# A two-block kernel's first twenty microseconds: silu(c) spread by TensorE, wider squares, products of ones, another order of loads

## The reference, cut to what matters

```python
cs = jax.nn.silu(c)                                  # c: 1 x 1024
shift, scale, gate = jnp.split(cs @ mod_w[layer] + mod_b[layer], 3, axis=-1)
h = rmsnorm(x, norm_g[layer]) * (1.0 + scale[:, None, :]) + shift[:, None, :]
u, g = jnp.split(h @ rg_w_in, 2, axis=-1)            # then conv, gates, linear recurrence, output product
```

## Time and profile before

| | |
|---|---|
| median of 3 runs | 742.0 us (741.99 to 742.11) |
| profiled execution | 742.27 us, its span 740.5 us |
| TensorE busy | 715.0 us, 97% of the span |
| VectorE, ScalarE busy | 502.9 us, 396.5 us |
| DMA, mean over the span | 212 GB/s |

### The profile page before, as it was taken

How to read it: one execution, slowest core, us unless ns; L and a number is a source line. 1 busy time by engine, 2 the same in 40 slices (tenths; PEclk the granted TensorE clock), 3 DMA queues, 4 the chain that set the end, 5 groups by cost and what they waited for, 6 DMA issues and landing times.

```text
span 740.5 us, 9710 instructions
## 1 busy us (share of the span) xinstructions
PE 715.0 (97%) x3902; PEld 625.0 (84%) x3902; DVE 502.9 (68%) x801; ACT 396.5 (54%) x620; POOL 2.4 (0%) x8
## 2 busy tenths in 40 slices
PE   2999999999999999999999999999999999999996
PEld 1888889999899999888888888888878888888885
DVE  4889996999876879976754454555576544555444
ACT  4156545883874776658734434443666344344423
POOL 0000000000000000000000000000000000000000
PEclk9999999999999999999999999999999999999999
DMA  8999994699835342433755545554336445545201
GB/s 336 419 422 415 421 385 163 250 393 340 316 118 216 116 170 71 182 111 150 271 183 183 208 177 177 207 185 171 114 114 227 171 173 208 187 173 201 81 0 58
DMA packets 23229, 156.65 MB, mean 212 GB/s; under 512 B 2576, under 2 KB 2832, under 8 KB 5264
## 3 DMA queue, kind: packets, MB, share of 16 engines
q1 hardware_dynamic: 22608, 153.41, 55.0%
q0 software_dynamic: 576, 2.62, 0.9%
HBM read 154.97 MB, written 1.05 MB: 211 GB/s over the span
## 4 chain that ended last, share of the span: by engine, by line
PE 86%; DVE 8%; ACT 4%; issue 1%; DMA 1%; SPq 0%; DVEq 0%
PE pb L1578 20%; PE pb L1580 20%; PE pb L1579 20%; PE pb L1642 13%; DVE w L1017 3%; DVE raw L1020 2%; PE pb L1852 2%; PE pb L1963 1%; PE pb L1719 1%; PE pb L1718 1%; PE pb L1720 1%; DMA x<-x_dram 1%; ACT w L624 1%; PE pb L1638 1%; PE pb L1885 1%
## 5 line engine op out<-in xcount | busy, mean ns | idle before, releaser
L1017 DVE TENSOR_TENSOR w<-raw,w 128x2048 fp32r<-128x2048 f32 x97 | 221.3, 2291 | 141.1 <-ACT w L624 141.1
L624 ACT ACTIVATE w<-raw 128x2048 fp32r<-128x2048 f32 x97 | 184.7, 1912 | 135.8 <-PE pb L1580 114.7
L1578 PE MATMUL pb<-w,r 128*128 128x512 f32 (+1 forms) x640 | 244.7, 382 | 0.7 <-DVE r L1020 0.3
L1580 PE MATMUL pb<-w,r 128*128 128x512 f32 (+1 forms) x640 | 241.1, 377 | 0.0
L1579 PE MATMUL pb<-w,r 128*128 128x512 f32 (+1 forms) x640 | 240.7, 376 | 0.0
L1578 PEld LDWEIGHTS pb<-w,r 128*128 128x128 f32 x640 | 120.5, 188 | 23.3 <-issue 2.1
L1580 PEld LDWEIGHTS pb<-w,r 128*128 128x128 f32 x640 | 120.4, 188 | 22.5
L1579 PEld LDWEIGHTS pb<-w,r 128*128 128x128 f32 x640 | 120.6, 188 | 21.0
L1578 PE MATMUL pb<-r,w 128*128 128x256 f32 x288 | 82.5, 287 | 0.4 <-DVE r L1017 0.4
L1579 PE MATMUL pb<-r,w 128*128 128x256 f32 x288 | 81.5, 283 | 0.0
L1580 PE MATMUL pb<-r,w 128*128 128x256 f32 x288 | 81.5, 283 | 0.0
(11 more groups left out here) (203 smaller groups left out, 657.2 us busy)
## 6 DMA issues: line engine op xcount, KB each, us to landing
raw<-w_dram SPq DMA_DIRECT2D x129, 1024.0 KB, 4.9
ow<-w_dram SPq DMA_DIRECT2D x8, 1024.0 KB, 14.2
ow<-w_dram SPq DMA_DIRECT2D x8, 512.0 KB, 17.0
oh<-w_dram SPq DMA_DIRECT2D x2, 1024.0 KB, 23.1
x<-x_dram SPq DMA_DIRECT2D x2, 512.0 KB, 6.1
f<-rc_dram POOLq DMA_DIRECT2D x1, 1024.0 KB, 5.1
acc<-row_dram POOLq DMA_DIRECT2D x2, 512.0 KB, 6.8
out_dram<-f SPq DMA_DIRECT2D x4, 256.0 KB, 2.3
```

Of the source, the lines that this page charges most:

```text
L624: return e.activation(out, in_, ACT.Copy, **kw)
L1017: return e.tensor_tensor(out, a, b, op)
L1578: e.matmul(out, a_hi, b_hi, start=start, stop=False)
L1580: return e.matmul(out, a_lo, b_hi, start=False, stop=stop)
```

## The change

- The load of c and its silu over 128x1024 go. The column silu(c), 128x8, which ScalarE computed already, is spread by TensorE: eight products with the identity into two banks, and VectorE copies the two banks of 128x512 into the same place (`silu_c`).
- The squares: one ScalarE instruction for tiles 0 to 3, two of two tiles each for the rest, into `F1`. VectorE adds two tiles at a time: three adds of 128x512 and one of 128x256, with the two copies of silu(c) between the first and the second.
- `first_close(0)` stands behind `first_tile(0)`. The table for the root is loaded before the squares.
- TensorE multiplies ones with ones where it has nothing to do: three products of 128x256 before the spreads of silu(c), four behind them, one behind the row sums and three behind the spread of the norm.
- The list of loads: first 0 and 1, u0, first 2, u1, first 3, u2, first 4, u3, first 5 and 6, u4, first 7, u5, u6, u7.

```diff
-    for kt in range(KT):
-        plan.extend([("first", "mod_w", 0, kt), ("u", "rg_w_in", 0, kt)])
+    for kind, kts in (("first", (0, 1)), ("u", (0,)), ("first", (2,)), ("u", (1,)), ("first", (3,)), ("u", (2,)),
+                      ("first", (4,)), ("u", (3,)), ("first", (5, 6)), ("u", (4,)), ("first", (7,)), ("u", (5, 6, 7))):
+        plan.extend((kind, "rg_w_in" if kind == "u" else "mod_w", 0, kt) for kt in kts)
...
     o = Outputs()
+    o.place(1, ("sc", 0))
+    o.place(2, ("sc", 1))
+    o.finish(("sc", 0), ("sc", 1))
...
             e.dma_start(cst[:, 0:P], cst_d[:, 0:P]).then_inc(s_id, 16)
-            e.dma_start(acc[0][:, :], c_d).then_inc(s_c, 16)
...
             e.activation(sm[:, 0, :], V("c", 0, 8), ACT.Silu).then_inc(s_cs, 1)
-            p.wait_ge(s_c, 16)
-            e.activation(silu_c, silu_c, ACT.Silu).then_inc(s_silu, 1)
-            for kt in range(KT):
-                if kt % 4 == 0:
-                    p.wait_ge((s_xa, s_xb)[kt // 4], 16)
-                e.activation(tt[kt][:, :], X[:, kt, :], ACT.Square).then_inc(s_sq, 1)
 
             e.activation(rn[:, 0, :], V("eps", 0, 2), ACT.Sqrt)
+            p.wait_ge(s_xa, 16)
+            e.activation(F1[:, 0:4, :], X[:, 0:4, :], ACT.Square).then_inc(s_sq0, 1)
+            p.wait_ge(s_xb, 16)
+            for kt in (4, 6):
+                e.activation(F1[:, kt:kt + 2, :], X[:, kt:kt + 2, :], ACT.Square).then_inc(s_sq0, 1)
...
-            e.memset(ones, 1.0).then_inc(s_ones, 1)
+            e.memset(ones, 1.0)
+            e.memset(sqt[0][:, :], 1.0).then_inc(s_ones, 1)
...
-            for kt in range(1, KT):
-                p.wait_ge(s_sq, kt + 1)
-                if kt > 1:
-                    p.wait_ge(s_n0, kt - 1)
-                tt_(tt[0][:, :], tt[0][:, :], tt[kt][:, :], ADD).then_inc(s_n0, 1)
+            two = F1[:, 0:2, :]
+            p.wait_ge(s_sq0, 1)
+            tt_(two, two, F1[:, 2:4, :], ADD).then_inc(s_n0, 1)
+            for c in range(2):
+                p.wait_ge(*ended("sc", c))
+                e.tensor_copy(silu_c[:, c * 512:c * 512 + 512], bank_of("sc", c)[:, :]).then_inc(s_silu, 1)
+            for n in range(1, 3):
+                p.wait_ge(s_sq0, n + 1)
+                p.wait_ge(s_n0, n)
+                tt_(two, two, F1[:, 2 * n + 2:2 * n + 4, :], ADD).then_inc(s_n0, 1)
+            p.wait_ge(s_n0, 3)
+            tt_(F1[:, 0, :], F1[:, 0, :], F1[:, 1, :], ADD).then_inc(s_n0, 1)
+            p.wait_ge(s_xb, 16)
             first_sums(0, [0])
             p.wait_ge(s_rt, 1)
             e.reciprocal(c0[:, :], c0[:, :]).then_inc(s_rc0, 1)
             first_sums(0, [1])
-            first_close(0)
             p.wait_ge(s_rs, 1)
             first_tile(0)
+            first_close(0)
...
+            def idle_products(n):
+
+                for _ in range(n):
+                    e.matmul(PB[5][:, 0:T], ones, sqt[0][:, :], start=True, stop=True)
+
+            p.wait_ge(s_ones, 1)
+            idle_products(3)
+
+            p.wait_ge(s_id, 16)
+            p.wait_ge(s_cs, 1)
+            for c in range(2):
+                bank_free("sc", c)
+                for j in range(4):
+                    done = spread(bank_of("sc", c)[:, j * P:j * P + P], sm[:, 0, 4 * c + j:4 * c + j + 1])
+                done.then_inc(s_ps, 1)
+            idle_products(4)
             bank_free("n", 0)
-            p.wait_ge(s_ones, 1)
-            p.wait_ge(s_n0, 7)
+            p.wait_ge(s_n0, 4)
             for a in range(2):
-                done = e.matmul(bank_of("n", 0)[:, a:a + 1], tt[0][:, a * P:a * P + P], ones_sb[:, 0:1], start=True,
+                done = e.matmul(bank_of("n", 0)[:, a:a + 1], F1[:, 0, a * P:a * P + P], ones_sb[:, 0:1], start=True,
                                 stop=True)
             done.then_inc(s_ps, 1)
-            p.wait_ge(s_id, 16)
+            idle_products(1)
             p.wait_ge(s_rc0, 1)
             bank_free("nr", 0)
             for a in range(2):
                 done = spread(bank_of("nr", 0)[:, a * P:a * P + P], c0[:, a:a + 1])
             done.then_inc(s_ps, 1)
+            idle_products(3)
```

More of the change, by code:

```diff
@@ L322, in wait_ge, with two_block_program @@
             self.met[id(sem)] = value
-def two_block_program(nc, w_d, vec_d, c_d, cst_d, dft_d, rcnt_d, row_d, x_d, out_d):
+def two_block_program(nc, w_d, vec_d, cst_d, dft_d, rcnt_d, row_d, x_d, out_d):
     f32, f32r = mybir.dt.float32, mybir.dt.float32r
@@ L380, in two_block_program @@
         s_own = [sem(f"s_own{n}") for n in range(len(OWN))]
-        s_vec, s_id, s_c, s_xa, s_xb, s_cst, s_dft, s_rc, s_prow, s_frow, s_out = (
-            sem(f"s_{n}") for n in ("vec", "id", "c", "xa", "xb", "cst", "dft", "rc", "prow", "frow", "out"))
+        s_vec, s_id, s_xa, s_xb, s_cst, s_dft, s_rc, s_prow, s_frow, s_out = (
+            sem(f"s_{n}") for n in ("vec", "id", "xa", "xb", "cst", "dft", "rc", "prow", "frow", "out"))
         s_hi, s_lo, s_mod, s_half = (sem(f"s_{n}") for n in ("hi", "lo", "mod", "half"))
@@ L390, in two_block_program @@
             sem(f"s_{n}") for n in ("ones", "pad", "gg", "cs", "silu", "lam", "sp", "one", "gain", "mv"))
-        s_n0, s_rc0 = sem("s_n0"), sem("s_rc0")
+        s_sq0, s_n0, s_rc0 = sem("s_sq0"), sem("s_n0"), sem("s_rc0")
         s_sq, s_na, s_rt, s_rs, s_rtc, s_rcl, s_rsb, s_xn = (
@@ L522, in freed @@
             i = at[0]
+            if kind == "sc":
+                return s_silu, i + 1
             if kind == "nr":
@@ L1034, in mod_sum @@
                 p.wait_ge(*landed(i))
-                p.wait_ge(s_silu, 1)
+                p.wait_ge(s_silu, 2)
                 for q in range(2):
@@ L1072, in add @@
             def add(j):
-                p.wait_ge(s_sq, 8 + j + 1)
+                p.wait_ge(s_sq, j + 1)
                 if j > 1:
@@ L1082, in two_adds @@
                     n = 2 * (d - 1) + m
-                    p.wait_ge(s_sq, 16 + 2 * d + m + 1)
+                    p.wait_ge(s_sq, 8 + 2 * d + m + 1)
                     if n >= 2:
@@ L2111 @@
     x = np.ascontiguousarray(a["x"][0].T.reshape(KT, P, T).transpose(1, 0, 2))
-    c = np.ascontiguousarray(np.broadcast_to(a["c"], (P, D)))
     rows = np.stack([a["pool_scale_2"].reshape(D), a["final_g_2"].reshape(D)])
     rows = np.ascontiguousarray(np.broadcast_to(rows[:, None, :], (2, P, D)))
-    arrays = {"w_dram": w, "vec_dram": vec, "c_dram": c, "cst_dram": cst, "dft_dram": dft, "rc_dram": rc,
+    arrays = {"w_dram": w, "vec_dram": vec, "cst_dram": cst, "dft_dram": dft, "rc_dram": rc,
               "row_dram": rows, "x_dram": x}
```

## The result

The changed kernel takes 743.7 us, the median of 12 runs (742.13 to 746.36), where the kernel before takes 742.0 (12 runs, 740.69 to 742.61): the ratio is 1.0027, 95% interval 1.0017 to 1.0036. It is slower by a little more than the 0.2% that a measurement tells from nothing. 741.3 was forecast, and the time lies outside the range, which ended at 743.6. What happened is rival B, the fall of the clock in the wait for u4, which was priced at 743.6 and given 0.17; on top of it the loads landed about 1 us later than counted.

What follows compares the result with a forecast made beforehand. TensorE was taken as the bound through stage u's end, with the order of loads deciding: 46.5 against 47.25 us, 0.75 gained, the wait costing no clock. Taking 0.7, 742.0 - 0.7 = 741.3 us; range 740.2 to 743.6.

Steps and rivals of the forecast that it cites:

- rival B: TensorE's wait for u slab 4: the clock falls, kt 4 starts at the low level; 743.6 us, chance 0.17.
- only the end of stage u counts: X times rg_w_in's first half on TensorE: each microsecond its last product ends earlier is one off the span.
- the list decides: Order of loads: u slab 4 lands at 32.3 us, kt 3 ends at 29.0; stage u ends 0.75 us earlier.
- The copies, squares and adds: Front, ahead of the row sums: with these at their priced times the sum is there at about 11.0 instead of 12.2 us.
- By the row the wait costs no clock: TensorE's 2.6 to 3.3 us wait before kt 4: the high level outlived over 3 us at program end; cost nothing.
- 13 records x 0.211 = 2.75 us: Price of a clock fall before kt 4, taken from the slow records at stage u's start in the earlier trace.
- c's 1.26 us: Load queue: without c's 512 KB, loads at the same place land 1.26 us earlier; the gain comes from this alone.
- the forecast 53.4: Start of the gates' first product, after stage u: near 53.4 us, against 54.16 before.
- Stage u's start: Its first product on TensorE: 15.1 us (high clock) to 15.7 us (low), against 16.75; the front gives 1.05 to 1.65.
- its two cases: Clock level in the front before stage u: high, with a start at 15.1 us, or low, with a start at 15.7.
- kt 3 would end at 31.7: Stage u: even with all its first steps at the low level, kt 3 ends at 31.7 us, ahead of u slab 4.
- By TensorE alone stage u would then end 4.5 us earlier: Stage u, if the ones raise the clock beforehand and loads do not bind: end at 42.75 us, 4.5 earlier.

Runs made afterwards that it cites:

- run 1: The changed kernel with the list of loads of the kernel before (first and u slabs alternating): 739.78 us, ratio 0.9981 to the kernel before.
- run 2: The kernel before with the changed list of loads, c still loaded: 742.67 us, ratio 1.0016 to the kernel before.
- run 10: The changed kernel once more, unchanged, for a second profile: 743.79 us.
- run 3: The changed kernel without its eleven products of ones: 742.37 us, ratio 1.0015 to the kernel before.
- 11: The changed kernel with a 512 KB load of an unused row where c's load was: 743.71 us.
- 9: The changed kernel with u0 ahead of first 1 in its list of loads: 743.31 us, ratio 1.0024 to the kernel before.
- run 4: The changed kernel with six products of ones with zeros between kt 3 and kt 4: 742.53 us, ratio 1.0011 to the kernel before.
- run 6: The kernel before with eighteen products of ones alone, c loaded, old squares and list: 740.54 us, ratio 0.9988 to the kernel before.

## Why the prediction was wrong

**Right.** That only the end of stage u counts: span minus the gates' first product is the same in all runs but one. That the list decides: u4's place gives a wait ahead of kt 4 that eats what the front and the clock gave (runs 1 and 2). The copies, squares and adds took no longer than priced: the row sums started at 11.53 where 11.0 was said, and x had landed 0.7 us later than said, at 6.62 instead of 5.9.

**The step that failed: "By the row the wait costs no clock".** The earlier trace rows show that the high level outlived the last product by over 3 us at the end of the program (the trace has 4.9, from 734.33 to 739.24), and from this one case the wait of 2.6 to 3.3 us was costed at nothing. The runs showed otherwise: with waits of 2.51 and 2.35 us for u4 the clock fell (the changed kernel, run 10), with waits of 1.76, 1.52, 1.26 and 1.03 us (runs 3, 11, 2, 9) it did not, and run 4, which only fills the wait, gives 1.2 us back. Without this term's 1.2 us the time would have been 742.5, inside the range. The Trainium skill's advice in TensorE: Matmul & The Clock Gate, "Why this matters for your kernels", to leave no long gaps between bursts of products, was cited and outvoted by a single row; the two falls in gaps of 2.51 and 2.35 us agree with it.

**The price of it.** Rival B had 13 records x 0.211 = 2.75 us, the number at the program's start. In the profile it was 7 records, 1.5 us. That B's sum, 743.6, still met the measured 743.7 is luck: its clock was priced 1.2 us too high, and u4 landed 1.0 us later than counted.

**The second term that failed: c's 1.26 us.** The forecast's whole gain was to come from it: u4 at 32.3 and u5 at 36.1 us. They landed at 33.30 and 37.06, u4 no earlier than in run 2, which still loads c. From the forecast 53.4 for the gates' first product to the 55.64 measured are 2.2 us. 1.0 of them is the late landing, which alone would have let kt 5 begin at 37.1; the other 1.2 is the clock, since of its 1.5 us kt 5 would have spent 0.3 waiting for u5 anyway (it began at 38.38, in run 4 at 37.26). So even with the clock right the change would have gained nothing: run 4 has 1.0011. The slabs before them show the same lag: u0 to u3 were counted at 14.3 to 25.5 us and landed at 15.59 to 27.07, and kt 2 and kt 3 had to wait for theirs.

**Stage u's start.** 15.1 to 15.7 us was said, 16.11 measured. Part is x's landing; the other part is the level, which had fallen around 12.5 us, after the wait for the row sums: the spread took 1.23 us, and the last three ones ran at the low price, for which 0.4 us had been named. That the level could rise and fall again inside the front was in neither of its two cases. Nor did the remark hold that kt 3 would end at 31.7 with all first steps at the low level: it counts from the start at the high level; from 15.7 it would be 32.3, no wait at all. In the changed kernel u3's landing set kt 3's end, and in run 3, with 7 records at the low level, it came at 30.85.

**The ones.** "By TensorE alone stage u would then end 4.5 us earlier" was rightly set against the loads: with the changed list kt 3 ended at 30.8 us both with the ones and without them (run 3). Run 3 is 0.9 us faster by the ratios, with intervals that overlap; in its profile u4 landed earlier and the clock did not fall, and the record does not tell whether the ones have a part in that.

## What to carry to other kernels

When a stage is fed by one saturated queue, count the bytes ahead of each slab before the list is reordered, and compare with the step that needs it: two slabs moved ahead of u4, and all first slabs ahead of u5, cost 3.4 us here, where the rest of the change gave 1.4. Making an engine faster up to a wait for a load gives nothing, and if the clock falls in the wait it costs; take the wait away by the order of the loads (3.4 us here), or fill it (1.2 us). And cost a wait of TensorE in the middle of a program by what the clock does after waits of its size; one stretch at the program's end is no price.

## What the runs showed of the hardware

The fall of the clock doesn't come at a fixed time after the last product. At the program's end it came 4.9 us after it. In the changed kernel the clock was at 0.50 from 33 us on, 2 us after kt 3's last product and before kt 4 began; in run 10 it was at 1.00 until kt 4 had already begun (33.18) and at 0.50 from 33.9 on. In run 6 it fell at 13.6 us, 1.5 us after TensorE had gone back to work from a wait of only 1.76 us, while a wait of that size inside stage u (run 3) left it alone. Ahead of the wait the work was dense in both; behind it came dense products in run 3, and in run 6 four records of one column, two records of ones and the four of the spread, with short gaps between. So with nearly the same wait the clock may or may not fall. That the runs of the changed kernel spread from 742.13 to 746.36, wider than those of the kernel before, may come from this in part: in the three fastest (742.13 to 742.59) the mean granted clock was 0.996 to 0.998, in seven (743.49 to 746.36) 0.992 to 0.994, but in two (743.58 and 744.01) it was 0.997. Where in them the clock fell was not recorded.
